# A two-layer trunk with gathered experts on one core: which steps run beside the u passes and which beside the v passes

## The chip, the cores and the metric

The kernel runs on one core of one Trainium2 chip. The metric is the time of one execution on the device in microseconds (us); lower is better. Three executions before the change took 2817.86, 2815.97 and 2802.0 us.

## What is computed

Two post-norm layers run over one prompt block (128 tokens, called P, block 0) and one sample of 256 tokens (called S, blocks 1 and 2 of 128 tokens each), with width 1024 in 32-bit floats. Each layer modulates its input, mixes tokens by three kinds of attention that share one input and one output projection, and then sends each token to 128 single-neuron experts out of 16,384. The sample attends to the cached context too. Cut to what matters:

```python
h   = layer_norm(x) * (1 + sc1) + sh1                    # sc, sh, g: from SiLU(cond) @ w_mod + b_mod
mix = concat(diff_attn, latent_attn, grouped_attn)(h @ w_in) @ w_out
x   = layer_norm(alpha * x + g1 * mix) * ln1_g + ln1_b
h   = layer_norm(x) * (1 + sc2) + sh2
s   = einsum('bshcd,hckd->bshck', h @ wq, keys)          # 8 heads, 2 halves, 128 keys
experts, gates = product_key_top16(s)                    # 8 heads * 16 = 128 experts a token
act = gelu(einsum('td,tkd->tk', h, u_tab[experts]))      # u rows: 128 per token
ff  = einsum('tk,tkd->td', gates * act, v_tab[experts])  # v rows: 128 per token
x   = layer_norm(alpha * x + g2 * ff) * ln2_g + ln2_b
```

## The kernel before

The experts' work is cut into six parts, (layer, block) = (0,0), (0,1), (0,2), (1,0), (1,1), (1,2). Each part has 128 **u passes** and then 128 **v passes**. A u pass gathers one row of `u_tab` per token (128 rows of 4 KB, an indirect DMA issued by GpSimd, L493) and VectorE (DVE) takes its dot product with the tokens' `h`, which lies in the two PSUM banks `acc` (L1177). A v pass gathers the rows of `v_tab`, with indices transposed so that the experts of one token lie across the partitions, and TensorE adds them, weighted through a diagonal strip, into the same `acc` (L738; two gathers make one step of four products). After each 64 u passes a `gelu` step turns dots into weights (L1184 to L1193); before each 64 v passes ScalarE writes the strip (`wdiag`, L911). Because both kinds use `acc`, the v passes of a part begin only after its last u pass, and the next part's u passes only after `fin` has read `acc` (L1203). All gathers go through one ring of 10 tiles (`expert`): gather i waits until pass i - 10 is done.

Beside the passes runs all work of the *next* part, cut into steps that carry a tuple of kind, layer, stream, block and piece:

- `ln1` (normalise and modulate), `h_t` (8 transposes), `win` (8 tiles of the input projection, 1 MB each), `prep` (norms of queries and keys, for the sample also rotary positions: four pieces a block), `k_t`, `cache_t`, `kv_mla` (transposed keys, the context's, and the latent keys and values). For the sample these are shared by blocks 1 and 2 and run once (`common_steps`).
- `q_t`, `q_rope`, `qm_t` (queries), `heads` (23 steps that pipeline 20 score matrices: product, maximum on DVE, exponential on ScalarE, transposes, product with the values), `mix`, `h_t`, `wout` (4 tiles of the output projection), `ln_x` (3 pieces), `ln_h` (2), `h_t`, `route` (9 steps, 8 tiles of router weights), `topk` (8) and `pick` (4: selection and gates), `idx_t`. These are a block's own (`block_steps`).
- `mod`: 4 tiles of 1 MB for each of a layer's six rows of modulation, for both layers.

`plan` writes one list of steps, `STEPS`, and every engine walks that one list in order and emits its share of each step. So the list fixes the order in every engine's queue, and an instruction that waits holds up what stands behind it on its engine. `weave` makes the list of one part: it deals 128 u and 128 v passes out among the steps by the estimated costs in `COST`. Before the change u passes go beside the first half of the cost and v passes beside the second half, whatever steps these are. The weight loads of SyncE (SP) are derived from the list as well: a tile is loaded as soon as the one three tiles earlier has been used for the last time.

The lines that the later sections speak of: L550 `h_t`, L560 `win`, L570 `wout`, L535 `mod`, L579 and L582 `k_t`, L616 `cache_t`, L626 and L630 `kv_mla`, L588 to L598 `q_t`, L609 `qm_t`, L650, L657 and L680 `heads` on TensorE, L702 and L711 `route`; on DVE L945 to L973 `prep`, L1052 the maxima of the heads, L1080 to L1088 `ln_x`, L1096 and L1097 `ln_h`, L1110 to L1129 `topk`, L1139 to L1167 `pick`.

Of the kernel before, what the change touches and what calls it, by code (L numbers as in the profile page):

```python
# [21 lines left out]
P = 128  # L22
# [10 lines left out]
SLOTS = R_HEADS * TOPK  # L33
# [8 lines left out]
IN_T = 8  # L42
# [12 lines left out]
HALF = SLOTS // 2  # L55
# [7 lines left out]
def lambda_init(l):  # L63
# [6 lines left out]
COST = {"mod": 4, "ln1": 3, "win": 7, "prep": 3, "k_t": 2, "q_t": 4, "q_rope": 1, "qm_t": 1, "cache_t": 2,  # L70
        "kv_mla": 5, "heads": 2.5, "mix": 3, "h_t": 2, "wout": 4, "ln_x": 3, "ln_h": 3, "route": 6.5, "topk": 2,
        "pick": 3, "fin": 3, "idx_t": 1}
# [11 lines left out]
def common_steps(l, s):  # L84

    out = []
    for b in BLOCKS[s]:
        out += [("ln1", l, s, b, 0), ("ln1", l, s, b, 1), ("h_t", l, s, b, 0)]
    out += [("win", l, s, n, 0) for n in range(IN_T)]
    for b in BLOCKS[s]:  # L90
        out += [("prep", l, s, b, i) for i in range(PREP_PIECES[s])] + [("k_t", l, s, b, 0)]
    if s == "S":
        out += [("cache_t", l, s, 0, 0)]
    return out + [("kv_mla", l, s, 0, 0)]


def block_steps(l, s, b):

    out = [("q_t", l, s, b, 0), ("q_rope", l, s, b, 0), ("qm_t", l, s, b, 0)]
    out += [("heads", l, s, b, i) for i in range(MATS + HEAD_TURNS)]  # L100
    out += [("mix", l, s, b, 0), ("h_t", l, s, b, 1)]
    out += [("wout", l, s, b, n) for n in range(OUT_T)]
    out += [("ln_x", l, s, b, i) for i in range(3)] + [("ln_h", l, s, b, i) for i in range(2)] + [("h_t", l, s, b, 2)]
    for n in range(WQ_T + 1):
        out += [("route", l, s, b, n)]
        if n >= 2:
            out += [("topk", l, s, b, n - 2)]
        if n - 2 == R_HEADS // 2 - 1:
            out += [("pick", l, s, b, i) for i in (0, 1)]
    return out + [("topk", l, s, b, R_HEADS - 1)] + [("pick", l, s, b, i) for i in (2, 3)] + [("idx_t", l, s, b, 0)]  # L110


def mod_steps(l, rows_=range(6)):
    return [("mod", l, "", row, c) for row in rows_ for c in range(MOD_T)]


def fill(steps, fillers, after):

    out, todo, due = [], list(fillers), 0
    for x in steps:  # L120
        out.append(x)
        due += after.get(x[0], 0)
        out += todo[:int(due)]
        todo, due = todo[int(due):], due % 1
    return out + todo


def weave(l, b, steps, turn=0.5):

    total = sum(COST[x[0]] for x in steps) or 1  # L130
    out, cost, u, v = [], 0, 0, 0

    def u_to(n):
        nonlocal u
        while u < n:
            at = min(n, u // HALF * HALF + HALF)
            out.append(("u", l, "", b, (u, at - u)))
            u = at
            if u % HALF == 0:
                out.append(("gelu", l, "", b, u // HALF - 1))  # L140

    def v_to(n):
        nonlocal v
        while v < n:
            at = min(n, v // HALF * HALF + HALF)
            if v % HALF == 0:
                out.append(("wdiag", l, "", b, v // HALF))
            out.append(("v", l, "", b, (v, at - v)))
            v = at

    for x in steps:
        out.append(x)
        cost += COST[x[0]]
        u_to(min(SLOTS, int(SLOTS * cost / (turn * total))))
        v_to(max(0, int(HALF * (cost - turn * total) / ((1 - turn) * total)) * 2))
    u_to(SLOTS)
    v_to(SLOTS)
    return out + [("fin", l, "", b, 0)]


def fin_rest(l, b):
    return [("fin", l, "", b, i) for i in (1, 2)]


def plan():
    steps = [("cond", 0, "", 0, 0)] + mod_steps(0, (0, 1))
    prompt = common_steps(0, "P") + block_steps(0, "P", 0)
    cut = prompt.index(("pick", 0, "P", 0, 1)) + 1
    between = {"ln1": 1, "prep": 1, "k_t": 1, "q_t": 1, "mix": 2, "ln_x": 1, "ln_h": 1}
    steps += fill(prompt[:cut], mod_steps(0, (2, 3, 4)), between)  # L170
    steps += weave(0, 0, prompt[cut:] + mod_steps(0, (5,)) + common_steps(0, "S") + block_steps(0, "S", 1))
    steps += weave(0, 1, fin_rest(0, 0) + block_steps(0, "S", 2) + mod_steps(1, (0, 1)))
    steps += weave(0, 2, fin_rest(0, 1) + fill(common_steps(1, "P") + block_steps(1, "P", 0), mod_steps(1, (2, 3, 4, 5)),
                                               between))
    steps += weave(1, 0, fin_rest(0, 2) + common_steps(1, "S") + block_steps(1, "S", 1))
    steps += weave(1, 1, fin_rest(1, 0) + block_steps(1, "S", 2))
    steps += weave(1, 2, fin_rest(1, 1)) + fin_rest(1, 2)
    return steps


STEPS = plan()


# [1113 lines left out]
```

## Time and profile before

| | before |
|---|---|
| runs, us | 2817.86, 2815.97, 2802.0 (median 2815.97) |
| profiled execution, us | 2809.33 |
| its span, us | 2807.5 |
| granted TensorE clock, mean | 0.781 |
| bytes moved by DMA | 1010 MB, 360 GB/s over the span |
| first u pass starts, us | 263.1 |

The span is the time from the first to the last profiled instruction; 1.8 us of the execution lie outside it. Times of stretches are counted from the start of the span. PE is TensorE, ACT ScalarE, POOL GpSimd, SP SyncE. A stage is the stretch from a part's first to last u pass (u0 to u5) or from its first to last v pass (v0 to v5).

### The profile page before, as it was taken

The numbers are of one execution on the slowest core, as the hardware profiler recorded it, in microseconds if no ns is written. First come the engines' busy times: TensorE is split into PE (matmuls) and PEld (weight loads), VectorE is DVE, ScalarE is ACT, GpSimd is POOL, SyncE is SP. The second block draws the span as 40 slices with busy tenths as digits, with TensorE's granted clock in tenths as the row PEclk, the third lists the DMA queues.
The fourth block names the chain that finished last, engine by engine and source line by source line (L and its number), as shares of the span: only waits on it lengthen the run. The fifth ranks groups of instructions, "written<-read, shape, count | busy, mean of one in ns | idle before, by whom it ended". The sixth has DMA issues, their size and how long they took to land.

```text
span 2807.5 us, 24172 instructions
## 1 busy us (share of the span) xinstructions
PE 1758.1 (63%) x8141; PEld 937.5 (33%) x8141; DVE 1670.6 (60%) x4099; ACT 265.3 (9%) x770; POOL 1469.6 (52%) x1541
## 2 busy tenths in 40 slices
PE   6875271799685487552689835298857558800476
PEld 2545061344254232141335334154424423300111
DVE  1236888525798742468813587953579854399401
ACT  1211000310021000000100000130002100000000
POOL 0002353555566466455645654455567656777674
PEclk9877685799855699776599967569985579955799
DMA  7556797889999999999999989689999999999997
GB/s 266 200 186 228 293 373 265 316 325 411 384 410 377 352 411 409 396 406 367 401 405 385 412 333 397 237 335 391 402 389 409 385 380 410 405 394 410 410 410 316
DMA packets 256425, 1010.06 MB, mean 360 GB/s; under 512 B 28912, under 2 KB 30592, under 8 KB 240944
## 3 DMA queue, kind: packets, MB, share of 16 engines
q0 software_dynamic: 221184, 805.40, 73.7%
q1 hardware_dynamic: 33344, 202.08, 18.4%
q8 instruction: 66, 1.08, 0.2%
q10 hardware_dynamic: 1776, 1.05, 0.1%
q14 instruction: 55, 0.45, 0.0%
HBM read 1005.80 MB, written 2.62 MB: 359 GB/s over the span
## 4 chain that ended last, share of the span: by engine, by line
DVE 32%; PE 28%; DMA 28%; POOL 6%; issue 4%; ACT 1%; ACTq 0%; SPq 0%; DVEq 0%; POOLq 0%
DVE expert L1177 19%; DMA expert<-in_experts,eidx_t 15%; PE acc L738 13%; DMA expert<-in_experts,eidx 11%; POOL expert L493 6%; PE mmb L702 4%; PE mmb L535 3%; PE mmb L570 2%; PE mmb L650 2%; PE ob L680 1%; DMA wt<-in_w_mod 1%; PE mmb L560 1%; PE trb L657 1%; DVE neg_max L1052 1%; DVE small L939 1%
## 5 line engine op out<-in xcount | busy, mean ns | idle before, releaser
L493 POOL DMA_INDIRECT expert<-in_experts,eidx x768 | 732.8, 954 | 799.7 <-DVE dots L1177 418.5
L493 POOL DMA_INDIRECT expert<-in_experts,eidx_t x768 | 734.8, 957 | 514.0 <-PE acc L738 329.5
L1177 DVE CUSTOM_DVE_ANT_0 expert<-expert,acc 128x1024 f32<-128x1024 f32 x768 | 904.4, 1217 | 98.5 <-DMA expert<-in_experts,eidx 84.7
L738 PE MATMUL acc<-expert,strip 128*32 128x512 f32 x3072 | 750.5, 622 | 160.2 <-DMA expert<-in_experts,eidx_t 154.6
L738 PEld LDWEIGHTS acc<-expert,strip 128*32 128x32 f32 x3072 | 177.9, 112 | 633.8 <-issue 616.9
L1110 DVE MAX8 router<-router 128x8 f32<-128x128 f32 x96 | 23.4, 285 | 306.6 <-ACT router L755 305.8
L702 PE MATMUL mmb<-hT,wt 128*128 128x128 f32 x1536 | 191.7, 285 | 13.4 <-ACT router L755 8.2
L702 PEld LDWEIGHTS mmb<-hT,wt 128*128 128x128 f32 x1536 | 183.1, 199 | 50.4 <-issue 36.7
L535 PE MATMUL mmb<-wt,csT 128*2 128x256 f32 x768 | 187.9, 405 | 17.5 <-DMA wt<-in_w_mod 17.3
L650 PE MATMUL mmb<-area 32*128 32x384 f32 (+5 forms) x240 | 137.9, 699 | 67.5 <-ACT area L863 63.0
L560 PE MATMUL mmb<-wt,hT 128*128 128x244 f32 x768 | 171.0, 387 | 8.2 <-DMA wt<-in_w_win 5.5
L560 PEld LDWEIGHTS mmb<-wt,hT 128*128 128x128 f32 x768 | 153.7, 201 | 25.6 <-issue 6.5
L721 PE MATMUL trb<-ident,acts 128*128 128x128 f32 x6 | 2.8, 474 | 225.9 <-DVE acts L1193 225.9
L579 PE MATMUL trb<-ident,wide 128*128 128x128 f32 x24 | 6.7, 434 | 208.0 <-DVEq L1038 208.0
L1203 DVE TENSOR_TENSOR tmp<-acc,rows 128x1024 f32<-128x1024 f32 x6 | 7.3, 1225 | 204.8 <-PE acc L738 204.8
L1052 DVE TENSOR_REDUCE neg_max<-mmb 128x1 f32<-128x384 f32 (+1 forms) x120 | 55.8, 466 | 101.8 <-PE mmb L650 101.7
L1008 DVE SCALAR_TENSOR_TENSOR wide<-wide 2x1024 f32<-2x1024 f32 x12 | 14.6, 1217 | 167.5 <-ACT wide L755 167.5
L535 PEld LDWEIGHTS mmb<-wt,csT 128*2 128x2 f32 x768 | 66.8, 89 | 130.6 <-issue 47.5
L570 PE MATMUL mmb<-wt,hT 128*128 128x256 f32 x384 | 97.1, 414 | 11.3 <-DMA wt<-in_w_wout 6.3
L550 PE MATMUL trb<-ident,tok 128*128 128x128 f32 x96 | 20.1, 378 | 118.9 <-DVE tok L1019 92.1
L570 PEld LDWEIGHTS mmb<-wt,hT 128*128 128x128 f32 x384 | 78.4, 208 | 33.9 <-issue 15.5
L755 ACT ACTIVATE router<-mmb 128x256 f32<-128x256 f32 x96 | 36.8, 384 | 536.2 <-PE mmb L702 471.4
(162 smaller groups left out, 1632.1 us busy)
## 6 DMA issues: line engine op xcount, KB each, us to landing
wt<-in_w_wq SPq DMA_DIRECT2D x48, 1152.0 KB, 8.3
wt<-in_w_mod SPq DMA_DIRECT2D x48, 1024.0 KB, 7.9
wt<-in_w_win SPq DMA_DIRECT2D x32, 976.0 KB, 8.0
wt<-in_w_wout SPq DMA_DIRECT2D x24, 1024.0 KB, 8.0
rows<-mod_scratch SPq DMA_DIRECT2D x32, 512.0 KB, 7.2
rows<-in_ln SPq DMA_DIRECT2D x24, 512.0 KB, 6.7
expert<-in_experts,eidx POOLq DMA_INDIRECT x768, 9.6
expert<-in_experts,eidx_t POOLq DMA_INDIRECT x768, 8.9
```

Source lines behind the costliest of these rows:

```text
L493: pool.indirect_dma_start(expert[:, g % RING, :], None, table, bass.IndirectOffsetOnAxis(at, 0)).then_inc(landed[g % RING], 16)
L535: m = pe.matmul(bank[0:2, 0:256], csT[:, :, kt], w[:, kt * 256:(kt + 1) * 256], start=kt == 0, stop=kt == KT - 1)
L560: m = pe.matmul(bank[:, jj * 256:jj * 256 + IN_C], hT[:, kt, jj * P:(jj + 1) * P], w[:, kt * IN_C:(kt + 1) * IN_C], start=kt == 0, stop=kt ...
L570: m = pe.matmul(bank[:, 0:256], hT[:, kt, cols], w[:, kt * 256:(kt + 1) * 256], start=kt == 0, stop=kt == KT - 1)
L650: pe.matmul(bank[:, 0:K], q_, k_, start=True, stop=True).then_inc(sc_full, 1)
L657: tr = pe.transpose(bank[:, kb * P:(kb + 1) * P], E[:, m % 2, kb * P:(kb + 1) * P], ident[:])
L680: o = pe.matmul(obank[:, (m % 8) * 64:(m % 8) * 64 + 64], ET[:, m % 2, kb * P:(kb + 1) * P], values(m, kb), start=kb == 0, stop=kb == KB - 1)
L702: m = pe.matmul(bank[:, i * P:(i + 1) * P], w[:, kt * 256 + i * P:kt * 256 + (i + 1) * P], hT[:, kt, cols], start=kt == 0, stop=kt == KT - 1)
L738: m = pe.matmul(acc[at:at + 32, cs], strip[:, i, 32 * c:32 * c + 32], expert[:, (g + i) % RING, cs], start=c == 0, stop=False, skip_group_ ...
L755: act.activation(dst, src_of(mmb[u % 2]), ACT.Copy).then_inc(mm_free, 1)
L1052: v.tensor_reduce(neg_max[:, m:m + 1], mmb[at_mm[m] % 2][:, 0:K], X, ALU.max, negate=True).then_inc(nmax_ready, 1)
L1177: v.tensor_tensor_reduce(expert[:, r, :], expert[:, r, :], acc[:], 1.0, 0.0, ALU.mult, ALU.add, dots[:, k:k + 1]).then_inc(dot_ready, 1)
```

## The change

Only the planner changes. `weave` takes two lists: steps to go beside the u passes and steps to go beside the v passes. Within each list passes are dealt out by cost as before. `plan` cuts each part's steps in one of two places: where the next block brings a new stream or layer, after its last `win` (so `ln1`, `h_t` and `win` go beside u; everything from `prep` on beside v); where it is the sample's second block, before its first `wout` (so queries, heads, `mix` and `h_t` go beside u). What was left of the prompt's selection at the start stays beside the u passes of part (0,0). In part (0,2) the modulation of layer 1 is divided anew: rows 2 and 3 beside u, rows 4 and 5 beside v. In the last part `fin` 2 moves ahead of the second 64 u passes.

```diff
-def weave(l, b, steps, turn=0.5):
-
-    total = sum(COST[x[0]] for x in steps) or 1
-    out, cost, u, v = [], 0, 0, 0
+def weave(l, b, during_u, during_v):
+
+    out = []
+    cost, done = sum(COST[x[0]] for x in during_u), 0
+    u = 0
...
+    for x in during_u:
+        out.append(x)
+        done += COST[x[0]]
+        u_to(int(SLOTS * done / cost))
+    u_to(SLOTS)
+
+    cost, done = sum(COST[x[0]] for x in during_v), 0
+    v = 0
...
-    for x in steps:
+    for x in during_v:
         out.append(x)
-        cost += COST[x[0]]
-        u_to(min(SLOTS, int(SLOTS * cost / (turn * total))))
-        v_to(max(0, int(HALF * (cost - turn * total) / ((1 - turn) * total)) * 2))
-    u_to(SLOTS)
+        done += COST[x[0]]
+        v_to(int(HALF * done / cost) * 2)
     v_to(SLOTS)
...
-    steps += weave(0, 0, prompt[cut:] + mod_steps(0, (5,)) + common_steps(0, "S") + block_steps(0, "S", 1))
-    steps += weave(0, 1, fin_rest(0, 0) + block_steps(0, "S", 2) + mod_steps(1, (0, 1)))
-    steps += weave(0, 2, fin_rest(0, 1) + fill(common_steps(1, "P") + block_steps(1, "P", 0), mod_steps(1, (2, 3, 4, 5)),
-                                               between))
-    steps += weave(1, 0, fin_rest(0, 2) + common_steps(1, "S") + block_steps(1, "S", 1))
-    steps += weave(1, 1, fin_rest(1, 0) + block_steps(1, "S", 2))
-    steps += weave(1, 2, fin_rest(1, 1)) + fin_rest(1, 2)
+
+    def to_win(l, s):
+        common = common_steps(l, s)
+        at = common.index(("win", l, s, IN_T - 1, 0)) + 1
+        return common[:at], common[at:]
+
+    def to_mix(l, s, b):
+        own = block_steps(l, s, b)
+        at = own.index(("wout", l, s, b, 0))
+        return own[:at], own[at:]
+
+    early, late = to_win(0, "S")
+    steps += weave(0, 0, prompt[cut:] + mod_steps(0, (5,)) + early, late + block_steps(0, "S", 1))
+    early, late = to_mix(0, "S", 2)
+    steps += weave(0, 1, fin_rest(0, 0) + early, late + mod_steps(1, (0, 1)))
+    early, late = to_win(1, "P")
+    steps += weave(0, 2, fin_rest(0, 1) + fill(early, mod_steps(1, (2, 3)), {"win": 1}),
+                   fill(late + block_steps(1, "P", 0), mod_steps(1, (4, 5)), between))
+    early, late = to_win(1, "S")
+    steps += weave(1, 0, fin_rest(0, 2) + early, late + block_steps(1, "S", 1))
+    early, late = to_mix(1, "S", 2)
+    steps += weave(1, 1, fin_rest(1, 0) + early, late)
+    steps += weave(1, 2, fin_rest(1, 1), []) + fin_rest(1, 2)
```

## Rows read from the trace of the kernel before

**Rows 1.** The page, its part 1: busy time and share of each engine.

```profile
PE 1758.1 (63%) x8141; PEld 937.5 (33%) x8141; DVE 1670.6 (60%) x4099; ACT 265.3 (9%) x770; POOL 1469.6 (52%) x1541
```

**Rows 2.** Stages u0, v0 to u5, v5: length; PE, PEld, DVE, ACT, POOL busy; PEclk, DMA share, GB/s.

```profile
263.10:524.40 261.30, 96.54 (x402) 70.40 (x402) 230.52 (x541) 22.49 (x62) 126.26 (x133) 0.66 0.84 320
530.00:753.20 223.20, 204.38 (x1072) 97.47 (x1071) 92.92 (x312) 27.90 (x77) 120.61 (x125) 0.97 0.95 363
760.90:957.60 196.70, 99.92 (x336) 72.38 (x336) 183.39 (x348) 26.33 (x71) 120.67 (x126) 0.55 0.98 380
965.80:1164.60 198.80, 163.67 (x870) 64.87 (x871) 64.19 (x238) 8.97 (x25) 119.33 (x126) 0.94 1.02 404
1172.20:1385.00 212.80, 86.97 (x329) 60.17 (x329) 178.99 (x353) 23.65 (x92) 120.35 (x127) 0.64 0.99 389
1387.90:1621.00 233.10, 207.36 (x1041) 90.77 (x1041) 86.07 (x295) 14.80 (x38) 122.58 (x126) 0.94 1.01 399
1628.60:1862.60 234.00, 111.46 (x434) 86.01 (x435) 207.17 (x435) 29.83 (x81) 121.79 (x127) 0.63 0.87 331
1868.20:2078.80 210.60, 185.63 (x973) 86.20 (x972) 87.36 (x301) 18.15 (x50) 121.15 (x126) 0.98 0.97 378
2086.50:2275.00 188.50, 92.89 (x296) 65.35 (x296) 176.88 (x330) 24.76 (x68) 120.95 (x127) 0.54 0.99 392
2277.80:2458.20 180.40, 157.22 (x809) 63.98 (x809) 67.27 (x253) 8.17 (x22) 118.85 (x124) 0.97 1.00 397
2465.80:2626.10 160.30, 0.00 (x0) 0.00 (x0) 154.40 (x261) 0.26 (x1) 118.91 (x127) 0.50 1.02 403
2629.00:2794.20 165.20, 126.17 (x512) 30.44 (x512) 1.10 (x1) 0.31 (x1) 110.71 (x118) 0.97 1.00 400
```

**Rows 3.** Single stretches, same columns: selection, `prep`, `win`, `ln_x` with `ln_h`, end of u3.

```profile
223.90:257.20 33.30, 22.05 (x184) 21.19 (x183) 30.81 (x118) 4.79 (x13) 0.08 (x1) 0.93 0.49 178
1743.40:1802.10 58.70, 1.33 (x5) 0.90 (x5) 54.59 (x158) 1.48 (x7) 19.77 (x21) 0.50 0.62 214
1670.00:1720.00 50.00, 49.69 (x242) 45.52 (x240) 36.30 (x62) 4.31 (x8) 29.90 (x32) 1.00 1.02 414
622.90:641.00 18.10, 11.74 (x48) 2.58 (x44) 16.06 (x38) 0.00 (x0) 11.98 (x11) 0.91 1.02 412
1828.00:1848.00 20.00, 19.10 (x57) 12.58 (x58) 19.17 (x35) 7.21 (x20) 13.06 (x14) 0.50 1.03 410
```

**Rows 4.** The `prep` stretch again, L1177 alone: length, DVE busy, PEclk, DMA share, GB/s.

```profile
1743.40:1802.10 58.70, 22.38 (x40) 0.50 0.62 214
```

**Rows 5.** PE in order of time in v0's route: start, us, engine, line.

```profile
668.33 5.34 PE L738 MATMUL acc<-expert,strip 128*32 128x512 f32 x24
673.60 3.84 PE L702 MATMUL mmb<-hT,wt 128*128 128x128 f32 x32
...
677.82 5.34 PE L738 MATMUL acc<-expert,strip 128*32 128x512 f32 x24
```

**Rows 6.** The same view in v3: one `wout` tile.

```profile
1929.52 3.72 PE L570 MATMUL mmb<-wt,hT 128*128 128x256 f32 x16
```

**Rows 7.** The same view in v0: two passes, one head step, the next passes.

```profile
562.66 1.91 PE L738 MATMUL acc<-expert,strip 128*32 128x512 f32 x8
564.50 0.91 PE L650 MATMUL mmb<-area 64*128 64x384 f32 x2
...
566.43 1.05 PE L738 MATMUL acc<-expert,strip 128*32 128x512 f32 x4
```

**Rows 8.** The same view in u0: first and last of `kv_mla` to `qm_t`.

```profile
501.89 4.29 PE L626 MATMUL mmb<-area,wt 128*64 128x384 f32 x8 [1.38 <-ACT area L843]
...
512.60 0.64 PE L609 MATMUL trb<-ident,area 128*96 128x128 f32 x4 [1.81 <-DVEq L1043]
```

**Rows 9.** The same view at the end of u0: a head step, then the first pass.

```profile
526.44 1.65 PE L650 MATMUL mmb<-area 32*128 32x384 f32 x2
...
530.02 2.57 PE L738 MATMUL acc<-expert,strip 128*32 128x512 f32 x6
```

## The prediction

> **What bounds the kernel now.** I read the page first, then the busy times of each engine in every stage, then the instruction order inside the stages. The page [rows 1] gives no answer: PE 63%, DVE 60%, no engine near its limit. The table by stage [rows 2] does. Each of the six parts (a layer's prompt block or one of its two sample blocks) has a u stage, in which VectorE takes 128 dot products, and a v stage, in which TensorE adds 128 gathered rows; the two cannot overlap, because both use `acc`. In the u stages of parts 0, 1, 3 and 4 (lines 1, 3, 7, 9 of the table) DVE is busy 88 to 94%, and TensorE 37 to 51% at a clock of 0.54 to 0.66. In the v stages (lines 2, 4, 6, 8, 10) it is the reverse: PE 82 to 92% at 0.94 to 0.98, DVE 32 to 42%. The third resource is the DMA: share 1.00 to 1.02 at about 400 GB/s in v1, v2, v4 and both stages of part 5, 0.97 to 0.99 in four more, but only 320, 363 and 331 GB/s in u0, v0 and u3. Part 5 has almost no work beside its passes: 160.3 and 165.2 us for 128 passes, 1.25 and 1.29 us a pass. That is the gathers' own pace, and no order of steps goes below it.
>
> So time can be won only where DMA is not full, and there by taking DVE work out of u or PE work out of v. The change does the first and the opposite of the second.
>
> **What moves.** No instruction is added or taken away (the same steps are dealt out anew). I counted the steps on either side of the first v pass by the cost table.
>
> *Parts 0 and 3* (next: the sample's shared steps and block 1). Out of u, into v: 8 `prep` pieces, 2 `k_t`, `cache_t`, `kv_mla`, `q_t`, `q_rope`, `qm_t`, and the first 5 (part 0) or about 13 (part 3) of 23 `heads` steps.
> - DVE price of the 8 preps: the stretch that holds them [rows 3] has 54.6 us of DVE (its second line), of which dot products 22.4 [rows 4]: 32.2 us. The DMA ran at 214 GB/s there: this is the hole the change closes. With q_rope (1) and the maxima of the heads (about 0.6 each) u0 loses 36 us of 230.5, u3 41 of 207.2.
> - Length of a DVE-bound u stage: stage over busy is 196.7/183.4 and 188.5/176.9, about 1.07. u0: 195 x 1.07 = 209, plus 4 for the wait at the last `mod` tile: 213 (before 261.3). u3: 166 x 1.07 = 178, but its bytes now bind. 331 GB/s x 234 us = 77.4 MB; it keeps all but two small tiles and two prefetched `wout` tiles, about 75.3 MB, and the best stretch ran at 414 GB/s (third line of [rows 3], where the projection stood): 184, I take 187 (before 234.0). Together -95 us.
> - PE prices at full clock: six passes 673.60 - 668.33 = 5.27, so 0.88 each; a route step 9.49 - 5.27 = 4.2 [rows 5]; a `wout` tile 3.7 [rows 6]; two passes and one head step 566.43 - 562.66 = 3.77, so 2.0 a head step [rows 7]. `kv_mla` to `qm_t` took from 501.89 to 513.2 [rows 8], about 11; the three transposing steps some 1 each.
> - The new v stage, identical in parts 0 and 3, piece by piece. (a) Preps: PE meets `k_t` of block 1 after 6 passes (5.3 us) and that of block 2 after 8 more; DVE needs 4 preps, 16.5 us, before each. The queue is in order, so the passes behind `k_t` wait too: 33 us for 14 passes, of which PE idles 19. (b) cache, kv, q, qm and 8 passes: 21. (c) 20 full heads at 2.0 and 32 passes: 68. (d) `mix`: 2 passes, 2 us wait: 4. (e) `h_t`, 4 `wout`, 8 passes, the copy into the strip: 25. (f) `ln_x`, `ln_h`: 18.1 us in the stretch that holds them (fourth line of [rows 3]), 10 passes beside it before, 8 now: 15 after (e). (g) `h_t`, eight routes (34), 52 passes (46): 82, and at the end two top-k and two pick steps of DVE against 8 passes. Four top-k and two picks take 30.8 us of DVE (first line of [rows 3]), so about 22 us against 7 and the last route: 10 us wait. Sum 33+21+68+4+25+15+92 = 258; 262 with a few us in which PE comes back at half clock after (a). Against before: v0 223.2, so +39; v3 210.6, so +51. The order of 10 gathers ahead hides none of it, since PE has no slack later to catch up.
> - Between u and v: 5.7 us before in both, now about 2.9, as in part 5: -3 each.
> Part 0: -48+39-3 = -12. Part 3: -47+51-3 = +1.
>
> *Parts 1 and 4* (next: block 2). Out of u, into v: three or four `wout`, `ln_x`, `ln_h` and `h_t` (part 1, with one route), or the `wout` and `ln_x` (part 4). u1 loses 16.1 us of DVE (fourth line of [rows 3]), u4 about 9.3 of them: both come to 167.5 x 1.07 = 180 (-17, -8). The v stages take over `wout` (15 PE) and some 2.7 MB. v1 is already at 404 GB/s: 80.4 + 2.7 = 83.1 MB, 206 us (+7). v4 has PE 157.2 of 180.4; +11 to 12 of it outside the gap, a longer `ln_x` chain with enough passes (16) beside it: 187 (+7). The first `wout` stands ahead of the first strip: gaps 6.9 (before 8.2 and 2.8): -1, +4. Part 1: -11. Part 4: +3.
>
> *Part 2* (next: layer 1's prompt). u2 was DMA bound (0.99, 389 GB/s) and gains two `mod` tiles: 208, -5. v2 gives two `mod` (3 us each) and takes 2 preps, k, kv, q, qm and nearly all 23 heads of the one-block kind (128 keys in place of 384, which I put at 0.7): PE 207 + 12 = 219. Preps here have two `mod` tiles beside them, so PE hardly waits; before, PE stood still for the `mod` row that now is stored earlier. 236, +3. Gap +4. Part 2: +2.
>
> Part 5 and the ends (the last part's `fin` 2 moves by 64 passes): 0. SP's order of loads follows the steps; the ring of 3 tiles stays, POOL's queue holds the same 1536 gathers, and the last picks stand before the last v passes as before.
>
> Sum: -12 -11 +2 +1 +3 = -17 us. The profiled execution took 2809.3 us around a span of 2807.5; the median of the runs is 2816.0, 7 us above it, inside their own spread of 16. I forecast 2816 - 16 = 2800 us.
>
> **Rivals.**
> - *The waits cost nothing* (chance 0.23). v3 idles 25 us already, mostly on gathers in its route stretch, and with 52 in place of some 80 passes there this idle time could absorb the 41 us of waits in (a), (d), (f), (g): v0 and v3 at about 235 to 240. For it: v3 is at 378 GB/s, near the gathers' pace. Against: the waits come first, the heads next, and v0's head stretch had PE busy throughout with one pass per 1.9 us. It would give -17 - 48, about 2750. It decides if v3 is below 240.
> - *DMA is the bound and bytes do not change* (0.12): what u stages gain comes back in the v stages, 2816. Mean rate after the gathers start is 375 GB/s, 410 in the best stretches; part 1's total could stay 404 us. The Trainium skill (DMA: Bandwidth & Descriptors, Specifications) gives about 358 GB/s of HBM per core, by which the kernel would be at its limit and no order could help. This case disagrees: 414 GB/s in a stretch of 50 us [rows 3].
> - *TensorE falls to half clock in the new v stages* (0.2), the slower side. At the end of u0 a head step without passes took 530.02 - 526.44 = 3.6 us, [rows 9], and PE 19 us busy of 20 still got 0.50 near the end of u3 (last line of [rows 3]). The preps now leave PE bursts of 5 to 8 us between waits of 9 to 10. If the half clock holds through (b) and (c), 20 heads cost 1.6 us more each (+32) and 32 passes at most 0.9 each: +30 to +60 in each of parts 0 and 3, so 2860 at the lower end; if it holds only over (b), about +10 each, 2820. It decides once the clock stays at 0.5 more than some 25 us into v. For it speaks u3's end; against, that v3 began with heads and passes mixed and its clock was 0.98. The Trainium skill (TensorE: Matmul & The Clock Gate, Part 1: The HAM clock gate) says throttled is the default and activity releases it, and warns of idle gaps; the rows agree with the first, and whether gaps filled by bursts count as idle no row here shows.
> - *Forecast* (0.45): 2775 to 2825.
>
> **Chances and range.** A measurement of this kernel can tell about 1%, 28 us, from no change. Faster by more: 0.23 and a tenth of the forecast's width, 0.3. Slower by more: most of the third rival, 0.18. Within: 0.52. The range takes in the first rival's centre and part of the third's: 2745 to 2850.
>
> **What would show it.** u0 213, u3 187, u1 and u4 180, u2 208 us; v0 and v3 equal within 3 us, at 262; two PE waits of 8 to 11 us for DVE at `k_t` (L579) at the start of each; v1 206, v2 236, v4 187; GB/s at 390 to 410 in u0 and u3, and down to about 310 in v0 and v3. It is wrong if v0 and v3 differ from 262 by more than 12, since two stages carry the error twice, or if the u stages of part 0 and 3 stay above 220 and 200.

## The result: slower by 0.65%, where 0.6% faster was forecast

| | before | after |
|---|---|---|
| median of ten runs, us | 2810.97 (2802.0 to 2817.86) | 2828.3 (2822.47 to 2833.92) |
| ratio of after to before | | 1.0065, 95% interval 1.0048 to 1.0083 |
| profiled execution: time, span, us | 2809.3, 2807.5 | 2828.09, 2826.3 |

The time lies within the predicted range (2745 to 2850), but the likeliest value, 2800, was on the wrong side of before: forecast -16 us, measured +17. That the range holds the result says little for the sum behind it, as the parts show.

The page of the changed kernel, its part 1, to be laid beside [rows 1]: PE has 37 us less of busy time, DVE 14 us more, and neither tells where 19 us of span went.

```profile
PE 1721.3 (61%) x8141; PEld 904.3 (32%) x8141; DVE 1684.4 (60%) x4099; ACT 265.1 (9%) x770; POOL 1460.9 (52%) x1541
```

The table by stage of the changed kernel, u0, v0 to u5, v5, with the columns of [rows 2] (length; PE, PEld, DVE, ACT, POOL busy; granted clock, DMA share, GB/s):

```profile
258.80:485.00 226.20, 76.17 (x337) 59.55 (x337) 198.01 (x416) 10.05 (x21) 124.76 (x132) 0.67 0.93 361
487.80:763.40 275.60, 230.14 (x1147) 109.98 (x1147) 128.70 (x433) 42.12 (x121) 121.76 (x126) 0.90 0.85 314
771.10:941.50 170.40, 73.83 (x232) 50.01 (x232) 167.85 (x310) 23.22 (x64) 118.49 (x127) 0.50 1.00 392
950.50:1165.60 215.10, 184.83 (x985) 82.21 (x985) 80.47 (x276) 12.31 (x33) 119.17 (x126) 0.94 1.01 403
1173.20:1382.00 208.80, 67.32 (x264) 39.91 (x264) 166.55 (x283) 7.32 (x19) 120.95 (x127) 0.67 1.01 404
1390.60:1620.60 230.00, 210.70 (x1124) 99.71 (x1124) 97.39 (x335) 31.43 (x112) 120.86 (x126) 0.99 1.01 398
1628.30:1819.20 190.90, 62.04 (x272) 55.19 (x272) 170.14 (x299) 7.04 (x13) 119.95 (x127) 0.64 0.98 379
1822.10:2094.80 272.70, 227.56 (x1147) 108.76 (x1147) 128.89 (x432) 42.11 (x121) 122.41 (x126) 0.92 0.85 316
2102.50:2272.60 170.10, 73.83 (x232) 50.03 (x232) 167.73 (x310) 23.21 (x64) 117.51 (x125) 0.50 0.99 389
2281.70:2475.80 194.10, 169.12 (x857) 72.60 (x857) 78.17 (x274) 9.49 (x25) 118.50 (x125) 0.96 1.01 396
2483.40:2647.20 163.80, 0.00 (x0) 0.00 (x0) 157.03 (x263) 0.26 (x1) 119.10 (x127) 0.50 1.02 403
2650.10:2813.00 162.90, 123.75 (x512) 29.91 (x512) 0.00 (x0) 0.32 (x1) 110.57 (x118) 0.99 1.00 396
```

Read by parts, each from its first u pass to its last v pass:

| part | before, us | after, us | measured | forecast |
|---|---|---|---|---|
| ahead of the first u pass | 263.1 | 258.8 | -4.3 | 0 |
| 0 | 490.1 | 504.6 | +14.5 | -12 |
| 1 | 403.7 | 394.5 | -9.2 | -11 |
| 2 | 448.8 | 447.4 | -1.4 | +2 |
| 3 | 450.2 | 466.5 | +16.3 | +1 |
| 4 | 371.7 | 373.4 | +1.6 | +3 |
| 5 | 328.5 | 329.6 | +1.1 | 0 |

The two parts with the large move carry the whole miss: +30.8 where -11 was forecast. The others came to -7.9, forecast -6. The stretch ahead of the first u pass has the same steps in both kernels and came out between 254 and 265 us in all profiles of this study, so its -4.3 is scatter.

Inside parts 0 and 3 the u stages gave back 35.1 and 43.1 us (forecast 48 and 47), the v stages took 52.4 and 62.1 (forecast 39 and 51), the gaps gave 2.8 and 2.7.

The next two views show v0 of the changed kernel: its busy times by piece (same columns), pieces (a), (b), (c) with (d), (e) with (f), and (g) in two, the lengths worked out in the prediction being 33, 21, 72, 40 and 92 us; then two stretches inside u0.

```profile
487.80:523.70 35.90, 17.43 (x61) 4.52 (x61) 31.92 (x112) 1.48 (x7) 14.22 (x14) 0.69 0.73 272
523.70:545.10 21.40, 18.78 (x73) 6.90 (x73) 1.03 (x4) 8.28 (x26) 6.55 (x7) 0.89 0.54 177
545.10:618.20 73.10, 71.04 (x365) 33.48 (x365) 17.79 (x43) 21.30 (x60) 33.71 (x36) 1.00 0.80 271
618.20:662.40 44.20, 33.57 (x144) 17.60 (x144) 16.13 (x38) 2.94 (x7) 18.64 (x19) 0.91 0.91 347
662.40:723.70 61.30, 57.71 (x348) 32.80 (x348) 34.73 (x138) 5.67 (x14) 28.93 (x30) 0.95 0.95 367
723.70:763.40 39.70, 31.62 (x160) 14.68 (x158) 27.09 (x99) 2.45 (x7) 19.70 (x20) 0.84 0.99 383
305.00:329.00 24.00, 0.13 (x1) 0.13 (x1) 22.91 (x58) 0.26 (x1) 6.55 (x7) 0.50 0.48 159
392.00:453.00 61.00, 56.11 (x259) 50.66 (x257) 47.70 (x80) 5.57 (x10) 36.53 (x39) 0.95 1.02 401
```

PE of the changed kernel in order of time (start, us, line, what, how many; in brackets the idle time before it and what ended it):

```profile
487.76 6.77 PE L762 MATMUL acc<-expert,strip 128*32 128x512 f32 x24 [0.71 <-ACT strip L935]
505.08 1.11 PE L603 MATMUL trb<-ident,wide 128*128 128x128 f32 x4 [10.54 <-DVEq L1062]
505.99 0.42 PE L606 MATMUL trb<-ident,wide 128*96 128x128 f32 x1
506.33 9.44 PE L762 MATMUL acc<-expert,strip 128*32 128x512 f32 x32
523.71 1.11 PE L603 MATMUL trb<-ident,wide 128*128 128x128 f32 x4 [7.94 <-DVEq L1062]
...
662.44 1.97 PE L574 MATMUL trb<-ident,h 128*128 128x128 f32 x8 [9.49 <-DVEq L1122]
...
721.45 2.35 PE L762 MATMUL acc<-expert,strip 128*32 128x512 f32 x8 [3.43 <-DMA expert<-in_experts,eidx_t]
...
752.79 2.97 PE L762 MATMUL acc<-expert,strip 128*32 128x512 f32 x8 [3.81 <-DMA expert<-in_experts,eidx_t]
759.38 0.48 PE L741 MATMUL trb<-ident,router 128*128 128x128 f32 x1 [3.62 <-DVEq L1191]
```

The waits at `k_t` are there as foretold, 10.5 us after six passes (24 records of `acc`, four to a pass) and 7.9 us after eight more, 18.5 us together. Over the 36 us of piece (a) DVE is busy for 32, most of it preps, and passes stand behind `k_t` in the queue that could have run: the gathers of the next four were issued before 486.4 us, and the gathers issued in this stretch landed 4.1 to 6.4 us after their issue. A third long wait, 9.5 us, is at the transposes behind `ln_h` (L574). So the mechanism was seen; the question for the runs is what the waits, the gathers and the plain work each cost.

### The profile page after: what moved, and what is told of

It reads as the page before. It is cut to its first block, busy times and chain, and to the rows that moved or that the text cites. A ratio compares the mean times of both kernels' runs of the same rounds, so it can differ in the third digit from the quotient of the medians.

```text
span 2826.3 us, 24158 instructions
## 1 busy us (share of the span) xinstructions
PE 1721.3 (61%) x8141; PEld 904.3 (32%) x8141; DVE 1684.4 (60%) x4099; ACT 265.1 (9%) x770; POOL 1460.9 (52%) x1541
## 4 chain that ended last, share of the span: by engine, by line
PE 31%; DVE 29%; DMA 29%; POOL 5%; issue 4%; ACT 1%; SPq 0%; ACTq 0%; DVEq 0%; POOLq 0%
DMA expert<-in_experts,eidx 17%; DVE expert L1201 15%; PE acc L762 14%; DMA expert<-in_experts,eidx_t 10%; POOL expert L517 5%; PE mmb L726 4%; PE mmb L594 3%; PE mmb L559 3%; PE mmb L674 2%; PE ob L704 1%; PE trb L681 1%; PE mmb L584 1%; DMA wt<-in_w_mod 1%; DVE small L963 1%; DVE newton L957 1%
## 5 line engine op out<-in xcount | busy, mean ns | idle before, releaser
L674 PE MATMUL mmb<-area 32*128 32x384 f32 (+5 forms) x240 | 121.4, 613 | 86.5 <-ACT area L887 82.1
L574 PE MATMUL trb<-ident,tok 128*128 128x128 f32 x96 | 19.3, 366 | 165.5 <-DVE tok L1043 128.8
L1104 DVE TENSOR_TENSOR tok<-tok,rows 128x1024 f32<-128x1024 f32 x6 | 7.3, 1225 | 160.9 <-ACT tok L779 160.9
L674 PEld LDWEIGHTS mmb<-area 32*128 32x128 f32 (+2 forms) x240 | 45.1, 241 | 134.3 <-ACT area L887 95.6
L594 PEld LDWEIGHTS mmb<-wt,hT 128*128 128x128 f32 x384 | 77.6, 206 | 30.8 <-issue 12.6
```

The lines of the kernel that those rows point to most:

```text
L594: m = pe.matmul(bank[:, 0:256], hT[:, kt, cols], w[:, kt * 256:(kt + 1) * 256], start=kt == 0, stop=kt == KT - 1)
L674: pe.matmul(bank[:, 0:K], q_, k_, start=True, stop=True).then_inc(sc_full, 1)
```

## The experiments

The device gave two levels of time. In e9 to e16 before took 2807.91 us (beside e9 to e12) and 2804.94 (beside e13 to e16), as in the result: level A. In e1 to e8 every kernel took about 5% longer, before 2943.09 us beside e1 to e4 and 2958.84 beside e5 to e8: level B, which has waits of its own (see the end). Each ratio is against before taken beside it, and six kernels were measured at both levels. The record numbers the chips 4, 7, 7 and 1 in the order of these four groups. Number 7 stands at both levels, so that the level belongs to a chip is not shown.

### Each half of the change alone

`shared_only` keeps the new split in parts 0 and 3 and takes back parts 1, 2 and 4 (its edit is shown); `second_only` keeps it in parts 1 and 4 and takes back parts 0, 2 and 3. Part 2 has its old order in both, so neither tests it. `weave_one` is the weave of before.

```diff
+def weave_one(l, b, steps, turn=0.5):
...
-    early, late = to_mix(0, "S", 2)
-    steps += weave(0, 1, fin_rest(0, 0) + early, late + mod_steps(1, (0, 1)))
+    steps += weave_one(0, 1, fin_rest(0, 0) + block_steps(0, "S", 2) + mod_steps(1, (0, 1)))
...
-    early, late = to_mix(1, "S", 2)
-    steps += weave(1, 1, fin_rest(1, 0) + early, late)
+    steps += weave_one(1, 1, fin_rest(1, 0) + block_steps(1, "S", 2))
```

> The new split only in parts 0 and 3 (next: the sample's shared steps), the old dealing in parts 1, 2 and 4. Theory (stretches inside a stage are bound in turn by DVE, PE and DMA, and only ten gathers can be carried over): the loss sits here, u0 and u3 about 226 and 191, v0 and v3 about 275 and 273 us, so 25 to 30 us slower than before. Rival (the loss is general, PE queues longer in every v stage): 10 us slower or less.

> The new split only in parts 1 and 4 (next: the sample's second block), old dealing in parts 0, 2 and 3. Theory: u1 and u4 about 170 us, v1 215, v4 194, so 7 to 10 us faster than before. Rival (the DMA is the bound and bytes do not change): the same as before within 3 us.

> The new split in parts 0 and 3 alone, on such a chip: the stages of the changed kernel there (part 0 +14, part 3 +16), 25 to 30 us slower than before.

> The new split in parts 1 and 4 alone, on such a chip: part 1 -9, part 4 +1, 5 to 10 us faster than before.

| run | us | ratio to before | stages |
|---|---|---|---|
| e1, parts 0 and 3 | 2947.34 | 1.0024 (1.0001 to 1.0046) | v0 269.4, v3 269.6 |
| e15, the same | 2833.96 | 1.0103 (1.0068 to 1.0138), +29 | v0 273.4, v3 274.2 |
| e2, parts 1 and 4 | 2938.63 | 0.9989 (0.9967 to 1.001) | v1 217.3, v4 201.1 |
| e16, the same | 2797.71 | 0.9974 (0.9961 to 0.9988), -7 | u1 170.1, v1 218.6, u4 169.9, v4 192.0 |

At level A (e15, e16) both came out as expected: +29 and -7 make +22, where the whole change, part 2 included, measured +17 to +18. So the change is a small gain in parts 1 and 4 and a larger loss in parts 0 and 3; part 2 moved by -1.4 us in the profile.

At level B, e1 missed its expectation: 4 us above before, as its rival had it, and e2 can't be told from no change. The stages v0 and v3 of e1 are nearly as long as expected, but before's u0 and u3 are so much longer there (293.9 and 271.4 us in e8) that taking work out of them gives back more: parts 0 and 3 of e1 come to 1009.6 us, those of e8 to 1013.1.

### The preps back beside the u passes

The cut stands ahead of `k_t` of block 2 in place of behind the last `win`.

```diff
-    early, late = to_win(0, "S")
+    early, late = to_prep(0)
...
-    early, late = to_win(1, "S")
+    early, late = to_prep(1)
```

> As the changed kernel, but in parts 0 and 3 the preps (DVE alone) stay beside the u passes; from the second k_t on everything stays beside v. Theory: u0 and u3 grow by 20 to 25 us each (32 us of DVE, part of it in room the DMA left), v0 and v3 lose the two waits of PE at k_t, 18 to 22 us each; total within 8 us of the changed kernel. Rival (half clock after the waits is what lengthens v0 and v3): v0 and v3 fall by 30 us or more each, the total by 15 or more.

Measured 2954.24 us, 1.0036 (1.0013 to 1.0058). v0 239.4 and v3 240.6 are 30 and 29 us shorter than in e1. That much the rival, half clock, had asked for, and it is more than the waits at `k_t`. The busy times of v0, of e1 and then of e3, in the columns of [rows 2], decide:

```profile
517.50:786.90 269.40, 224.30 (x1147) 107.48 (x1148) 128.79 (x433) 41.46 (x121) 122.55 (x126) 0.93 0.84 312
545.30:784.70 239.40, 223.18 (x1132) 107.14 (x1133) 97.27 (x321) 36.81 (x100) 119.35 (x126) 0.95 0.91 342
```

PE's busy time fell by 1 us and its idle time by 29, from 45.1 to 16.2. The two waits at `k_t` (10.3 and 9.3 us in e1) are gone; the wait at the transposes behind `ln_h` fell from 9.5 to 0.6 us and the one before `idx_t`, 3.1 us, is gone too, for the 14 passes that stood beside the preps now stand further behind. So it was waiting and not the clock.

The time is paid back ahead of the first v pass: from the first u pass to it are 286.9 us in part 0 and 249.2 in part 3, in e1 261.6 and 209.1. The 32 us of DVE work of the eight preps cost 25 and 40 us there.

### The preps kept beside the v passes, with more passes between them

The weave deals passes to steps in proportion to the cost table, and a prep had a cost that gave it 2 passes where it takes 4 us of DVE.

```diff
+PREP_LONG = {**COST, "prep": 7}
...
-    steps += weave(0, 0, prompt[cut:] + mod_steps(0, (5,)) + early, late + block_steps(0, "S", 1))
+    steps += weave(0, 0, prompt[cut:] + mod_steps(0, (5,)) + early, late + block_steps(0, "S", 1), PREP_LONG)
```

> As the changed kernel, but in the v stages of parts 0 and 3 a prep counts 7 in place of 3 when passes are dealt out: 28 passes stand beside the preps in place of 14, fewer behind. Same work, same split. Theory (an in-order PE queue waits for late DVE work, and PE cannot make it up): v0 and v3 lose most of the 19 us of waits at k_t and get back 5 us at the picks: 10 to 15 us each, total 20 to 30 us faster than the changed kernel, so about 5 us faster than before. Rival (the waits are hidden, PE or DMA work alone sets v0): within 5 us of the changed kernel.

Measured 2929.01 us, 0.9952 (0.9937 to 0.9967); v0 264.7, v3 259.6, in e1 beside it 269.4 and 269.6. That is 5 and 10 us, where 10 to 15 each was expected. At one and the same split between u and v, the number of passes ahead of a wait moves the stage.

### Both kernels again, at either level

> The changed kernel itself, so that what runs beside it is compared on one chip. On a chip where the kernel before takes about 2810 us: 15 to 20 us slower. On one like that of the four runs before (2943 us, with waits of PE and ACT that no instruction or DMA releases): equal within 5 us.

> The kernel before itself, one look, so that its stages stand beside those of the others on the same chip. On a fast chip u0, v0, u3, v3 261, 223, 234, 211 us as before; on a slower one longer in the u stages.

> The changed kernel once more, for the comparison on this call's chip: 15 to 20 us slower than before on a fast chip (2810 us before), equal within 5 us on one like that of the last two calls.

e5: 2960.51 us, 1.001 (0.9992 to 1.0027); e8: 2952.36 (one run). e12, at level A: 2825.78 us, 1.0061 (1.0044 to 1.0078), v0 273.5, v3 274.4. So at level B the two kernels can't be told apart, and at level A the +17 of the result stands.

### Passes dealt by what the steps take in v

```diff
+V_COST = {"prep": 3.2, "k_t": 0.6, "cache_t": 0.6, "kv_mla": 1.6, "q_t": 1.6, "q_rope": 0.5, "qm_t": 0.5, "heads": 1.15,
+          "mix": 2, "h_t": 0.8, "wout": 1.6, "ln_x": 2.8, "ln_h": 2.8, "route": 2, "topk": 1.5, "pick": 3, "idx_t": 0.5}
+V_LATE = {("topk", R_HEADS - 2): 4, ("topk", R_HEADS - 1): 4.5, ("pick", 2): 5, ("pick", 3): 5}
...
     for x in during_v:
         out.append(x)
-        done += COST[x[0]]
+        done += price(x)
```

This puts 24 passes beside the preps in place of 14 and 12 beside `ln_x` and `ln_h` in place of 8, and leaves 22 behind the last `route` in place of 10, in parts 0 and 3 alone. `dealt_mod` also moves the four `mod` tiles of u0 from behind the prompt's last steps to among its top-k steps:

```diff
-    steps += weave(0, 0, prompt[cut:] + mod_steps(0, (5,)) + early, ...
+    steps += weave(0, 0, fill(prompt[cut:], mod_steps(0, (5,)), {"topk": 1}) + early, ...
```

> As the changed kernel, same split, but the v passes of parts 0 and 3 are dealt out by prices of their own: about as many passes beside a step as DVE keeps PE waiting for it (24 passes beside the preps in place of 14, 12 beside ln_x and ln_h in place of 8, 20 from the last route on in place of 8) and fewer beside heads, wout and routes. Theory (waits for DVE in PE's in-order queue, and the DMA idle while PE stands in heads, full afterwards): v0 and v3 from 275 to about 243 us each, total 50 to 65 us below the changed kernel. Rival (PE work alone fills v0 and v3): within 10 us.

> As the last one, and the four mod tiles of row 5 (4 MB of loads) stand among the prompt's four top-k steps, where u0 is bound by DVE and the DMA is half idle, in place of behind them. Theory (u0 is first bound by DVE and then by DMA, and nothing is carried across): u0 from 226 to about 216 us, total 8 to 10 us below the last kernel. Rival (the sum of DVE work over the stage sets u0): no change.

> The kernel with own v prices again, hoped to fall on a chip on which the kernel before takes about 2810 us. There, from the stages seen so far (v0 and v3 255 to 258 in place of 273 to 276): 30 to 36 us below the changed kernel, so 0.4 to 0.7% faster than before. Rival (the gain came only from the slower chip, where u0 ends in a 40 us gap): within 10 us of the changed kernel, slower than before.

> The same with the mod tiles among the top-k steps: another 5 to 10 us, from u0 alone (226 to 216 to 221).

| run | us | ratio to before | u0 | v0 | v3 |
|---|---|---|---|---|---|
| e6 | 2936.01 | 0.991 (0.9886 to 0.9933) | | 255.2 | 257.8 |
| e13, the same | 2787.16 | 0.9941 (0.9925 to 0.9957) | 226.2 | 253.7 | 254.9 |
| e7, with the `mod` tiles moved | 2931.98 | 0.9895 (0.987 to 0.9919) | 213.7 | 258.0 | 257.2 |
| e14, the same | 2788.12 | 0.9937 (0.9916 to 0.9958) | 223.6 | 255.0 | 252.3 |

e13 is faster than both kernels: 17.8 us below before, 39 to 41 below the changed one. The profiles agree with the times: v0 is 21.9 and v3 17.8 us shorter than after, 39.7 together. Of the 21.9 us in v0, 17.0 are idle time of PE (45.5 to 28.5) and 4.9 busy time. The busy times of e13, first v0, then its first piece (preps) and its last:

```profile
483.00:736.70 253.70, 225.21 (x1147) 107.35 (x1147) 129.16 (x433) 41.91 (x121) 121.58 (x126) 0.95 0.89 332
483.00:519.40 36.40, 26.05 (x101) 6.55 (x101) 32.46 (x112) 1.48 (x7) 24.39 (x23) 0.88 0.96 358
704.50:736.70 32.20, 25.26 (x109) 6.70 (x107) 22.25 (x76) 1.69 (x5) 20.32 (x22) 0.95 1.02 411
```

And PE of e13 at the two `k_t` steps:

```profile
500.50 0.66 PE L612 MATMUL trb<-ident,wide 128*128 128x128 f32 x4 [4.23 <-DVEq L1071]
...
519.45 1.12 PE L612 MATMUL trb<-ident,wide 128*128 128x128 f32 x4 [6.01 <-DVEq L1071]
```

The preps take 36.4 us as before the new dealing (35.9), but 24 passes come out of them in place of 14. The waits at `k_t` shrank from 18.5 to 10.2 us, and the one behind `ln_h` from 9.5 to 1.0. I had expected 243 us for v0, not 253.7, and 50 to 65 us below the changed kernel in e6, which gave 24.5: the waits at `k_t` did not vanish, and the last piece, with 24 passes, runs at 411 GB/s, the gathers' pace, so passes saved up for the end cost their rows' transfer there. Moving the `mod` tiles brought 2.6 us in u0 in e14, with a first u pass 6.7 us later; e14 took 1 us more than e13 where 5 to 10 less were expected, so no gain can be read from it.

One control was not run: the old split with its passes dealt by such prices. So e13 shows that the dealing turns this split from a loss into a gain. It doesn't show how much of the 0.6% is the split's.

### Half of each gathered row

Here the gathers bring 2 KB in place of each 4 KB row, so the DMA has slack while every instruction of DVE and PE stays. The other half of each ring tile is left at zero, and the tables are cut into rows of 512: the kernels compute other numbers, and only their times are read.

```diff
-            table = t_in["experts"].rearrange("e (h d) -> (e h) d", h=2)
+            table = t_in["experts"].rearrange("e (h d) -> (e h) d", h=4)
...
-                    pool.indirect_dma_start(expert[:, g % RING, :], None, table, bass.IndirectOffsetOnAxis(at, 0)
+                    pool.indirect_dma_start(expert[:, g % RING, 0:D // 2], None, table, bass.IndirectOffsetOnAxis(at, 0)
```

> The kernel before with half of every gathered row left out: each gather fetches 2 KB per partition in place of 4 (the first 512 columns, from a table seen as rows of 512, so other numbers), the rest of the ring tile is a zero written once at the start, and all arithmetic stays. This takes the gathers' bytes away and leaves DVE and PE work and their waits. Theory: stages fall to the engine that bounds them, u0 and u3 about 241 and 215 (DVE), v0 and v3 212 and 195 (PE), u5 158, v5 115.

> The changed kernel with the same halving of the gathers (same part left out). Theory (the waits for DVE and PE's own work set v0 and v3, the DMA adds the rest in the route stretch): u0 206, u3 174, v0 and v3 about 262 each, so parts 0 and 3 together still 20 us or more longer than in the halved kernel before. Rival (the uneven load on the DMA is what the change loses by): v0 and v3 fall below 245, and parts 0 and 3 together are shorter than in the halved kernel before.

Before comes to 2623.65 us, after to 2661.43 (one run each): +37.8, twice the difference with full rows. u0, v0 and v2, of half before and then of half after, in the columns of [rows 2]:

```profile
258.00:505.80 247.80, 98.72 (x417) 72.16 (x415) 228.51 (x541) 22.87 (x63) 128.74 (x134) 0.68 0.62 206
511.40:726.50 215.10, 201.95 (x1072) 97.33 (x1072) 93.09 (x312) 27.85 (x77) 122.10 (x126) 0.98 0.70 226
1298.00:1503.50 205.50, 197.15 (x1041) 89.54 (x1041) 86.06 (x295) 14.69 (x38) 122.22 (x125) 0.98 0.84 284
```

```profile
254.60:454.30 199.70, 77.18 (x351) 60.85 (x349) 193.47 (x416) 10.44 (x22) 123.17 (x130) 0.70 0.72 240
457.10:726.70 269.60, 227.29 (x1147) 108.85 (x1147) 128.86 (x433) 42.06 (x121) 126.45 (x129) 0.92 0.61 193
1291.10:1521.10 230.00, 211.45 (x1124) 99.99 (x1124) 97.74 (x336) 31.37 (x112) 121.80 (x126) 0.96 0.77 258
```

| stage | half rows: before, after | full rows: before, after |
|---|---|---|
| u0 | 247.8, 199.7 (-48) | 261.3, 226.2 (-35) |
| v0 | 215.1, 269.6 (+54) | 223.2, 275.6 (+52) |
| u3 | 214.1, 167.3 (-47) | 234.0, 190.9 (-43) |
| v3 | 195.9, 269.7 (+74) | 210.6, 272.7 (+62) |
| u2 | 188.2, 175.2 (-13) | 212.8, 208.8 (-4) |
| v2 | 205.5, 230.0 (+24) | 233.1, 230.0 (-3) |
| part 2 | 396.8, 413.6 (+17) | 448.8, 447.4 (-1) |

The new v0 and v3 hardly feel the transfers: 6 and 3 us. Their 270 us are PE's work and waits. With the gathers halved u0 loses the 48 us of the forecast; with full rows, 13 less. And part 2's order costs 17 us that the gathers hide: its v2 takes 230.0 us with either rows, so PE and its waits have become the bound there, while the v2 of before, 233.1 us, was bound by the gathers.

### One prep only beside the u passes

Only block 1's preps stay in u (here `to_prep` cuts ahead of the first prep of block 2), with the passes dealt and the `mod` tiles as in e14.

```diff
-    early, late = to_win(0, "S")
+    early, late = to_prep(0)
```

> As the kernel with own v prices and mod tiles among the top-k steps, and block 1's four preps and its k_t stay beside the u passes of parts 0 and 3 (16 us of DVE each), block 2's go beside v. Theory (the DMA-bound second half of u0 has some 15 us of DVE to spare, and v0 loses one wait of about 8 us and the passes dealt beside it): u0 and u3 +8 to +16 us, v0 and v3 -16 to -18 each, total 5 to 15 us below that kernel. Rival (u stages have no room): equal or slower.

Measured 2816.35 us, 1.0034 (1.0018 to 1.005), 28 us above e14 where 5 to 15 below it was expected, and so the rival's way; against e14 u0 is 17.2 and u3 some 17 us longer, v0 and v3 4 us shorter each (250.6, 248.1). Four preps in u cost what DVE takes for them, 16.5 us by the prediction's own price; out of v they save a fourth of it once passes lie beside them.

## Why the prediction was wrong, by its own steps

**Right.** DVE's busy time in u0 fell by 32.5 us (36 foretold), and with the gathers halved u0 shortened by the 48 us predicted. The waits at `k_t` were foretold at 8 to 11 us and are 10.5 and 7.9; v0 and v3 were to be equal within 3 us, and are (275.6, 272.7). u3 190.9 (187), u2 208.8 (208), v2 230.0 (236; a `mod` tile took 3.7 us of PE in v2 of before, where 3 was put), the gaps within 2.2 us. The new v stages run at 314 and 316 GB/s (310). In parts 1 and 4 two errors cancel, which is luck: u1 and u4 are 170 us, not 180, for DVE is busy for 167.9 of 170.4 and the factor 1.07, read off stages of before, did not hold (why isn't tested; PE is busy for 73.8 us there and was for 99.9); v1 and v4 are 215.1 and 194.1, not 206 and 187, both at the gathers' pace (403 and 396 GB/s).

**The first wrong step: TensorE's work in the new v stage, mostly in "(e)" and "(g)", and with it the sum 258.** The stages are 275.6 and 272.7. By its own test ("wrong if v0 and v3 differ from 262 by more than 12") the forecast falls with v0: it is 13.6 off, and v3 10.7, which make 24 of the 42 us missed in parts 0 and 3. The pieces measured: (a) 35.9 against 33, (b) 21.4 against 21, (c) and (d) 73.1 against 72, (e) and (f) 44.2 against 40, (g) 101.0 against 92. The sum had 217 us of PE and 41 of waits; the trace has 230.1 and 45.5. So the waits were sized about right and the work was not.

The term at fault is the passes. PE's busy time in them over v0, of the changed kernel and then of before (length; PE, PEld; granted clock, DMA share, GB/s):

```profile
487.80:763.40 275.60, 128.28 (x512) 27.59 (x512) 0.90 0.85 314
530.00:753.20 223.20, 124.13 (x512) 27.95 (x512) 0.97 0.95 363
```

That is 1.00 us a pass, and was 0.97 before. The prediction priced a pass at 0.88, from six in a row at full clock, and its pieces hold 124 of the 128: (c) and (d) have 34 where the trace has 36 (144 records), (e) and (f) 16 where it has 18 (72). It came to 109 us, 19 short; all other PE work came out some 6 us below its prices.

Begun at v0's measured PE busy time, 204.4 us [rows 2], the sum is 204.4 + 9.1 (PE's busy time from `kv_mla` to `qm_t`, the stretch of [rows 8]) + 3 (three transposing steps) + 10 (five heads) = 227, and with the 41 us of waits 268. It should have started there and not have built the old work anew. Of the 8 us then left, 4 are PE's work, beside a mean clock of 0.90 in place of 0.97 (the same 128 passes took 4.2 us more), and 4.5 idle time, beside the waits for gathers of 3.4 and 3.8 us in (g).

**The second: u0 213.** It is 226.2, another 13 us, above the 220 that the prediction named as its other sign of being wrong, and the rate is 361 GB/s in u0 and 379 in u3 where 390 to 410 was foretold. The prediction let DVE's work bound the whole of u0, though DVE and the bytes bind in turn. In the stretch 305:329 of u0 DVE has steps of its own, the passes wait for it, and the DMA moves 159 GB/s; in 392:453 the projection's tiles come beside the gathers and it is at 401. The ring of ten gathers carried little from the first into the second, so the lengths add. e9 and e10 show the size: halved rows take 13.5 us off u0 of before and 26.5 off the new one. For u3 I did take the bytes, and it was off by 4 (75.3 MB at 414 GB/s are 182 us and not 184; 187 was taken, so nothing hangs on it). That another order inside u0 would win this back isn't shown: moving the `mod` tiles gave 2.6 us.

**The rivals.** *The waits cost nothing* is refuted: v0 stayed at 269.6 with the transfers halved, and passes laid beside the waits took 22 and 18 us off v0 and v3 without moving a step between u and v. *DMA is the bound* is true of v1, u2 and v4 (share 1.01), which halved rows shorten by 27, 34 and 24 us, and in part 2 it hid 17 us. It is false of v0 and v3, of u1 and u4 (1.7 and 1.1 us shorter with halved rows: DVE bounds them), and of the new v2, which shows a share of 1.01 as well and yet takes 230.0 us with either rows. *TensorE falls to half clock* had the time nearly right (2820 at its lower end) for a reason that did not occur: the clock was 0.69 over the 36 us of (a), in which PE waits for DVE anyway, 0.89 in (b), and 1.00 in (c), where it was to cost 32 us. With more passes in (a) it was 0.88 (e13). The Trainium skill (TensorE: Matmul & The Clock Gate, Part 1: The HAM clock gate) has activity release the clock; the two rows on the same 36 us, 0.69 with 14 passes and 0.88 with 24, agree. That the clock isn't what lengthens v0 and v3 shows in e3: with the waits gone, PE's busy time is within 1 us of e1's.

**Where the expected gain went**, then: of the 48 us that DVE's relief was worth in u0, 13 to the gathers; the rest of parts 0 and 3 to v stages that took 115 us where 90 were forecast. The before kernel had v3 waiting 15 us for gathers (210.6 against 195.9 with half rows), and the new order does use that slack, but puts 74 us of work and waits into it.

## What to carry to other kernels

When steps are moved between two stages with different bottlenecks, what is paid is the work in the new stage plus every wait at which the in-order queue holds back ready work; deal the filler work by how long the other engine takes for each step, in that stage, before judging the split. Here the split alone lost 0.65%, and the same split with the passes dealt anew won 0.6%. Price a changed stage from its measured busy time, plus and minus what moves, and count the filler work. Split a stage at the points where its bottleneck changes: here the bounds of successive stretches added, for a ring of ten transfers levelled little out. And a full share of the DMA doesn't prove that it is the bound; a run with fewer bytes does.

## What the runs showed of the hardware

At level B the same programs took 5% longer. There u5 of before, the stage at the gathers' pace, took 174.1 us (160.3 in [rows 2]), and u0 and u3 took 293.9 and 271.4 (261.3 and 234.0). In u5 of before at that level (e8, DVE in order of time) these dot products start 1.40 us apart with 0.17 us ahead of each that nothing ended:

```profile
2618.81 1.22 DVE L1177 CUSTOM_DVE_ANT_0 expert<-expert,acc 128x1024 f32<-128x1024 f32 x1 [0.17 <-issue]
2619.95 0.08 DVE L1177 DVE_READ_ACCUMULATOR2_ANT dots<- 128x1 f32 x1
2620.21 1.22 DVE L1177 CUSTOM_DVE_ANT_0 expert<-expert,acc 128x1024 f32<-128x1024 f32 x1 [0.17 <-issue]
```

In the changed kernel there (e5) DVE stood at the end of u0, its `tanh` result late, and v0 began 42.5 us after u0 (2.8 in the result):

```profile
478.92 0.22 DVE L1210 TENSOR_TENSOR gelu<-gelu,dots 128x64 f32<-128x64 f32 x1 [0.53 <-DVE gelu L1209]
514.67 0.22 DVE L1216 SCALAR_TENSOR_TENSOR gelu<-gelu,dots 128x64 f32<-128x64 f32 x1 [35.52 <-ACT gelu L925]
```

The projection's matmuls were late there with nothing that the profile names ahead of them. What makes the level is open; no run here tells. It shows that a ratio of 1.0065 at one level can be 1.001 at another, and that the better dealing kept its gain at both (0.9941 and 0.991).
